# Moving one more group of channels of a depthwise convolution from VectorE to ScalarE and GpSimd, and summing its channels on VectorE, in a two-block model on one Trainium2 core

## What is computed

```python
def conformer_conv_module(h, w_in, b_in, dw, dw_b, ln_g, ln_b, w_out, b_out):
    u = h @ w_in + b_in
    u = u[..., :D_MODEL] * jax.nn.sigmoid(u[..., D_MODEL:])
    u = causal_dwconv(u, dw, dw_b)      # 31 taps, one filter per channel
    u = layer_norm(u, ln_g, ln_b)       # mean and variance over the 1024 channels
    u = jax.nn.silu(u)
    return u @ w_out + b_out
```

## Time and profile before

| | |
|---|---|
| median of 3 runs | 2315.63 us (2314.86 to 2317.98) |
| the profiled execution, its device time | 2316.43 us |
| the profiled execution, its span (first to last instruction) | 2314.6 us |
| TensorE busy | 2261.3 us, 98% |
| VectorE busy | 766.3 us, 33% |
| ScalarE busy | 430.4 us, 19% |
| GpSimd busy | 44.0 us, 2% |
| mean granted TensorE clock | 0.997 of 2.4 GHz |
| DMA | 639.71 MB, mean 276 GB/s |

### The profile page before, as it was taken

How to read it: one execution, slowest core, us unless ns; L and a number is a source line. 1 busy time by engine, 2 the same in 40 slices (tenths; PEclk the granted TensorE clock), 3 DMA queues, 4 the chain that set the end, 5 groups by cost and what they waited for, 6 DMA issues and landing times.

```text
span 2314.6 us, 31523 instructions
## 1 busy us (share of the span) xinstructions
PE 2261.3 (98%) x12908; PEld 1712.2 (74%) x12908; DVE 766.3 (33%) x1859; ACT 430.4 (19%) x1031; POOL 44.0 (2%) x66
## 2 busy tenths in 40 slices
PE   9999999999999999999999999999999999999998
PEld 8888888888888888888887885555555555555555
DVE  7944342433053441210647632222222121112212
ACT  3542210201033211110235121111111111111112
POOL 0700000000000000000000000000000000000000
PEclk9999999999999999999999999999999999999999
DMA  9644446668424444336532659999999999999996
GB/s 395 226 146 146 146 181 237 218 227 309 174 90 157 156 161 146 128 126 229 157 107 73 259 205 381 427 426 428 427 429 427 429 427 429 428 428 427 425 428 293
DMA packets 65976, 639.71 MB, mean 276 GB/s; under 512 B 7464, under 2 KB 9896, under 8 KB 12624
## 3 DMA queue, kind: packets, MB, share of 16 engines
q1 hardware_dynamic: 65872, 638.25, 69.6%
HBM read 630.86 MB, written 4.21 MB: 274 GB/s over the span
## 4 chain that ended last, share of the span: by engine, by line
PE 79%; DMA 14%; DVE 6%; issue 1%; ACT 0%; DVEq 0%; SPq 0%
PE bank L701 27%; PE bank L1283 15%; DMA arena<-in_experts 9%; PE bank L698 6%; PE bank L803 5%; PE bank L1320 5%; DMA ring<-in_experts 4%; PE bank L715 3%; PE bank L690 3%; DVE bank L2013 3%; PE bank L1274 2%; PE bank L1242 1%; PE bank L1230 1%; PE bank L814 1%; PE bank L761 1%
## 5 line engine op out<-in xcount | busy, mean ns | idle before, releaser
L701 PE MATMUL bank<-arena,ring 128*128 128x256 f32 x3136 | 680.3, 379 | 0.0
L701 PEld LDWEIGHTS bank<-arena,ring 128*128 128x128 f32 x3136 | 595.4, 190 | 80.7
L2430 DVE TENSOR_SCALAR arena<-bank 128x256 f32<-128x256 f32 x64 | 27.1, 424 | 676.2 <-PE bank L1283 676.2
L1283 PE MATMUL bank<-arena 128*64 128x256 f32 x2048 | 231.3, 380 | 12.9 <-DMA arena<-in_experts 12.8
L1283 PE MATMUL bank<-ring,arena 128*64 128x256 f32 x2048 | 234.1, 383 | 6.6 <-DMA ring<-in_experts 6.6
L1283 PEld LDWEIGHTS bank<-ring,arena 128*64 128x64 f32 x2048 | 143.3, 138 | 112.4 <-issue 30.3
L1283 PEld LDWEIGHTS bank<-arena 128*64 128x64 f32 x2048 | 144.3, 137 | 101.5 <-DMA arena<-in_experts 21.1
L698 PE MATMUL bank<-ring,arena 128*128 128x256 f32 x608 | 132.0, 379 | 0.0
L698 PEld LDWEIGHTS bank<-ring,arena 128*128 128x128 f32 x608 | 115.4, 190 | 15.6
L1732 ACT ACTIVATE arena<-arena 128x256 f32<-128x256 f32 x64 | 26.7, 416 | 532.9 <-DVE arena L2430 532.9
L803 PE MATMUL bank<-arena,ring 128*128 128x256 f32 x576 | 124.6, 379 | 0.0
(11 more groups left out here) (323 smaller groups left out, 2063.4 us busy)
## 6 DMA issues: line engine op xcount, KB each, us to landing
ring<-in_dense SPq DMA_DIRECT2D x203, 1024.0 KB, 4.9
arena<-in_experts SPq DMA_DIRECT2D x96, 2048.0 KB, 31.4
ring<-in_experts SPq DMA_DIRECT2D x87, 2048.0 KB, 30.9
ring<-in_experts SPq DMA_DIRECT2D x16, 1024.0 KB, 32.9
arena<-park SPq DMA_DIRECT2D x3, 1024.0 KB, 7.4
arena<-in_dense SPq DMA_DIRECT2D x2, 1024.0 KB, 19.1
park<-ring SPq DMA_DIRECT2D x2, 1024.0 KB, 8.2
ring<-arena SPq DMA_DIRECT2D x16, 128.0 KB, 5.6
```

The costliest lines, as they stand in the source:

```text
L701: ins = nc.tensor.matmul(o, w[:, k, j * P:(j + 1) * P], src[:, k, :], start=(k == 0), stop=(k == KT - 1))
L1283: ins = nc.tensor.matmul(o, XGT[:, k, e * CAP:(e + 1) * CAP], w[:, k, :], start=False, stop=(k == KT - 1), skip_group_check=True)
```

## The change

Chunk 5 goes from VectorE to ScalarE and GpSimd, so that VectorE has chunks 0 to 4 and the others 5 to 7. GpSimd gates the three chunks with one instruction of 768 columns and adds one tap of all three with one instruction of 768 columns, 30 in all, each by `me(...)`, waiting for itself. The ring of products stays four taps deep, now of three chunks each, in `Y` and `SQ`. ScalarE computes 93 products in place of 62, five taps behind each early unit in place of four. VectorE runs chunks 0, 1 as a pair and chunks 2, 3, 4 as a triple, with the three gatings ahead of the triple; then it adds the eight chunks into `TMP` (`channels`, seven additions, each waiting for the one before; the last three wait for GpSimd's last tap), so that TensorE needs one matmul for the mean. Of the squares of chunks 0 to 5 VectorE makes one sum (`presum`, five additions), so that TensorE needs three matmuls in place of eight. The mean's matmul stands in the middle of early unit 7, the squares' three behind the first half of unit 8.

```diff
-POOL_CHUNKS = (6, 7)
+POOL_FIRST = 5
+POOL_CHUNKS = KT - POOL_FIRST
+POOL_RING = 4
...
+        def tap_places(k):
+
+            at = (k - 1) % POOL_RING
+            return (Y, SQ)[at // 2][:, at % 2 * POOL_CHUNKS:(at % 2 + 1) * POOL_CHUNKS, :]
...
+            def channel_mean():
+
+                pe.wait_ge(sem("channels"), KT - 1)
+                nc.tensor.matmul(banks[WORK][:, 0:T], mean, TMP[:, 0:T], start=True, stop=True)\
+                    .then_inc(sem("ln_mean"), 1)
...
-            for n in range(6):
+            for n in range(EARLY - 2):
                 early(n)
-            for c in range(4):
-                channel_sum(c)
-            for n in range(6, EARLY - 1):
-                early(n)
+            early(EARLY - 2, (0,))
+            channel_mean()
+            early(EARLY - 2, (1,))
             early(EARLY - 1, (0,))
-            for c in range(4, KT):
-                ins = channel_sum(c)
-            ins.then_inc(sem("ln_mean"), 1)
-            stat("ln", 1, mean)
+            part_summed("ln", 1)
             early(EARLY - 1, (1,))
...
-            tap_products(0, 5)
-            for n in range(EARLY - 1):
+            tap_products(0, POOL_RING + 1)
+            for n in range(EARLY - 2):
                 early_out(n)
-                tap_products(5 + 4 * n, min(9 + 4 * n, TAPS))
+                tap_products(5 + 5 * n, min(10 + 5 * n, TAPS))
...
             square("ln", lambda c: U[:, c, :], "ln_centred")
+            early_out(EARLY - 2)
             root("ln", 1)
...
-            for c in POOL_CHUNKS:
+            for c in range(POOL_FIRST, KT):
                 unit_half(pool, FIRST_UNIT["cm_in"] + c, 2)
-                me.do(nc.gpsimd.tensor_tensor(G[:, c, TAPS - 1:], G[:, c, TAPS - 1:], SG[:, c, :], ALU.mult))
+            me(nc.gpsimd.tensor_tensor(G[:, own, TAPS - 1:], G[:, own, TAPS - 1:], SG[:, own, :], ALU.mult))
             for k in range(1, TAPS):
-                for i, c in enumerate(POOL_CHUNKS):
-                    pool.wait_ge(sem("tap_product"), 2 * k + i + 1)
-                    me.ended(me.n - 1)
-                    me.do(nc.gpsimd.tensor_tensor(U[:, c, :], U[:, c, :], tap_place(k, i), ALU.add))
+                pool.wait_ge(sem("tap_product"), POOL_CHUNKS * (k + 1))
+                me(nc.gpsimd.tensor_tensor(U[:, own, :], U[:, own, :], tap_places(k), ALU.add))
...
+            def channels():
+
+                me.ended()
+                for c in range(1, KT):
+                    if c == POOL_FIRST:
+                        dve.wait_ge(sem("pool_steps"), TAPS)
+                    if c > 1:
+                        dve.wait_ge(sem("channels"), c - 1)
+                    V.tensor_tensor(TMP[:, 0:T], U[:, 0, :] if c == 1 else TMP[:, 0:T], U[:, c, :], ALU.add)\
+                     .then_inc(sem("channels"), 1)
...
-            conv(0, beside)
-            glu(2)
-            glu(3)
-            conv(2, {4: [(glu, (4,)), (glu, (5,))]})
-            conv(4)
+            conv((0, 1), beside)
+            for j in range(2, POOL_FIRST):
+                glu(j)
+            conv(range(2, POOL_FIRST))
+            channels()
             dve.wait_ge(sem("ln_mean"), 1)
...
+            presum("ln", end=KT - 2, to="_part")
             r = rstd("ln", 1)
```

More of the change, by code:

```diff
@@ L779, in part_spread, with part_summed @@
                 fill(n, 4, 2 * KT)
-            def part_summed(name):
+            def part_summed(name, half=0):
                 for n, c in enumerate((0, KT - 2, KT - 1)):
@@ L787, in part_summed @@
                         pe.wait_ge(sem(name + "_part"), before(name + "_part") + KT - 3)
-                    ins = nc.tensor.matmul(banks[STAT][:, 0:T], mean, SQ[:, c, :], start=(n == 0), stop=(n == 2))
+                    ins = nc.tensor.matmul(banks[STAT][:, half * T:(half + 1) * T], mean, SQ[:, c, :],
+                                           start=(n == 0), stop=(n == 2))
                 ins.then_inc(sem(name + "_sum"), 1)
@@ L1515, in tap_products @@
                 for k in range(first, end):
[L1516 to L1524 removed]
+                    if k == 0:
+                        act.wait_ge(sem("pool_steps"), 1)
+                    elif k > POOL_RING:
+                        act.wait_ge(sem("pool_steps"), 1 + k - POOL_RING)
+                    for i in range(POOL_CHUNKS):
+                        c = POOL_FIRST + i
+                        nc.scalar.activation(tap_places(k)[:, i, :] if k else U[:, c, :], G[:, c, k:k + T], ACT.Identity,
+                                             scale=par_col("cm_dw", k * 8 + c),
                                              bias=par_col("cm_dw_b", c) if k == 0 else 0.0).then_inc(sem("tap_product"), 1)
[L1527 to L1528 removed]
+            tap_products(0, POOL_RING + 1)
+            for n in range(EARLY - 2):
                 early_out(n)
[L1530 removed]
+                tap_products(5 + 5 * n, min(10 + 5 * n, TAPS))
                 if n == 0:
@@ L1998, in glu, with conv @@
                 V.tensor_tensor(G[:, j, TAPS - 1:], G[:, j, TAPS - 1:], SG[:, j, :], ALU.mult).then_inc(sem("glu"), 1)
-            def conv(c, between={}):
-                dve.wait_ge(sem("glu"), c + 2)
+            def conv(chunks, between={}):
+                dve.wait_ge(sem("glu"), chunks[-1] + 1)
                 for k in range(TAPS):
@@ L2005, in conv @@
                         step(*arg)
-                    for i in range(2):
-                        w, src = par_col("cm_dw", k * 8 + c + i), G[:, c + i, k:k + T]
-                        kept = banks[6 + c // 2 % 2][:, i * T:(i + 1) * T]
+                    for c in chunks:
+                        w, src = par_col("cm_dw", k * 8 + c), G[:, c, k:k + T]
+                        kept = banks[6 + c // 2 % 2][:, c % 2 * T:(c % 2 + 1) * T]
                         if k == 0:
-                            me.do(V.tensor_scalar(kept, src, w, par_col("cm_dw_b", c + i), ALU.mult, ALU.add))
+                            me.do(V.tensor_scalar(kept, src, w, par_col("cm_dw_b", c), ALU.mult, ALU.add))
                             continue
-                        me.ended(me.n - 1 if k < TAPS - 1 else me.n - 1 + i)
-                        ins = V.scalar_tensor_tensor(kept if k < TAPS - 1 else U[:, c + i, :], src, w, kept, ALU.mult, ALU.add)
-                        if k < TAPS - 1:
-                            me.do(ins)
-                        else:
-                            ins.then_inc(sem("conv"), 1)
+                        me.ended(me.n - len(chunks) + 1)
+                        me.do(V.scalar_tensor_tensor(kept if k < TAPS - 1 else U[:, c, :], src, w, kept, ALU.mult, ALU.add))
+            def channels():
[7 more added lines that the diff above has]
+                     .then_inc(sem("channels"), 1)
             raw_unit(0)
```

12 lines of the change are left out of this document (2 added, 10 removed).

## The result

The changed kernel takes 2324.17 us (median of 9 runs, 2321.86 to 2324.61); the kernel before took 2316.61 beside it (9 runs, 2314.62 to 2318.68). The ratio is 1.0028, with an interval from 1.0019 to 1.0038: slower by 4.4 to 8.8 us (1.0028 is 6.5 us; the two medians themselves are 7.6 apart). The forecast was 2320.2, the range 2315 to 2326.5.

What follows compares the result with a forecast made beforehand. VectorE's convolution was taken to bound this stage before, GpSimd's additions after the change. A later mean (+1.9 us) and the clock's fall (+2.7) gave +4.6: 2320.2 us against the median 2315.63, range 2315 to 2326.5.

Steps and rivals of the forecast that it cites:

- the bounds 1.5 and 2.23: Lower and upper ends, in us, for GpSimd's addition of 768 columns; 1.83 was taken.
- rivals 1 and 2: GpSimd's 768-column addition takes 2.03: 2326 us, chance 0.16; or 1.5: 2310.6 us (2313.3 with a clock fall), chance 0.07.
- The contention term: VectorE operations with two SBUF operands delay GpSimd's additions by 0.18 us each, four channel additions counted.
- T: The time at which the mean's matmul starts on TensorE: 129.7 us, with the output product 12.2 us later.
- its 1.9: Cost of the mean's later start by itself, in us: T of 129.7 less the break-even of 127.8.
- Its two waits: TensorE's waits ahead of the second four channel sums and the sums of squares, to vanish: 2.7 us.
- the bound of 2.1: Upper end, in us, for one VectorE channel addition if it waits for GpSimd's running 768-column addition; lower end 0.51.
- The squares' chain: Centring, squares and their additions beside TensorE's two halves end at T + 6.2: no cost, 1.1 us of cover.
- The clock: TensorE's 10 us wait halves its granted clock for some five microseconds of work behind it: 2.7 us more.
- rival 3: T as forecast, but TensorE's clock stays up or returns within a microsecond or two: +1.9 to +3, 2318 us, chance 0.09.
- rival 4: The delay is swallowed before or in the phase in which weights bound: 2316 us, chance 0.06.
- of "within" and "slower": Outcomes for the whole kernel: within 0.2% of before, chance 0.46; slower by over 0.2%, chance 0.47.

Runs made afterwards that it cites:

- the version with three additions a tap: The changed kernel with GpSimd's 768-column addition split into three of 256, each waiting for the instruction before the previous one: 2328.83 us, 1.0051.
- all three profiles: The changed kernel, unaltered, profiled in three separate measurements: 2324.17, 2324.04 and 2323.11 us, ratios 1.0028, 1.0029 and 1.0027.
- wait filled: The changed kernel with twenty throwaway matmuls on TensorE in the wait ahead of the mean's matmul: 2320.73 us, 1.0014.
- The balanced version: The changed kernel with gatings early, VectorE taking chunk 5 for the last 12 taps, channel sums on TensorE in mid unit 7: 2313.31 us, 0.9983.
- the sums alone: The kernel before, chunks unmoved, with the change's channel and squares' sums on VectorE and its TensorE order: 2324.43 us, 1.0032.
- the four of higher clock above: Four of ten executions of the changed kernel with VectorE's three gatings moved into the first pair's taps: 2319.7 to 2320.3 us, mean clock 0.996 or 0.997.

## Why the prediction was right, and where it was not

Times are given from the start of the early products, 63.98 in the profile of before.

- **What bounds.** Right: GpSimd's last tap sets the mean. Its addition takes 1.82 (forecast 1.83), the reaction 0.08 (0.10). Of the bounds 1.5 and 2.23 neither was near, so rivals 1 and 2 fall by that one row. The products ahead of the first addition took 0.3 longer, and the last tap ended at 63.1 in place of 64.1: a tap was 1.906 with all that held it up, forecast 1.95. The contention term was too large for GpSimd: beside VectorE's gatings and channel additions its addition takes 1.86 to 1.88, some 0.05 more in place of 0.18. The 0.18 came from additions that overlap and holds for those: in the version with three additions a tap, three of them take 0.91 in place of 0.73 beside the gatings.
- **T.** 64.5 in all three profiles, forecast 65.7 (129.7). The wait ahead of the mean is 8.97, forecast 10.3. The way from there to the output product is 12.4 at full clock, forecast 12.2. The forecast's own balance of its 1.9 doesn't close: 10.3 less 5.2 and 2.7 is 2.4. Its two waits are 2.6 by the rows, and counted from start to start the time that TensorE lost there is 3.2, which gives the 1.9; the sum was worked out by the starts, so it isn't touched.
- **VectorE.** The three gatings took 5.78 (5.5). The fourth channel addition ended 1.69 ahead of GpSimd's last tap, where the forecast had anything from 0.3 to 6.6 ahead (and 0.5 behind by the Trainium skill's rule). The four lasted 1.77 on average, near the bound of 2.1, and each ended 0.28 behind the end of one of GpSimd's additions. So the hold-up is a wait for the running addition, as the Trainium skill has it (SBUF — State Buffer, Who interferes with whom). It was not waited for, as forecast.
- **The squares' chain** costs nothing, right: with the clock up (wait filled) VectorE ends them at 137.92 and the sums start at 139.43, 1.5 of cover where I had 1.1.
- **The clock.** Right in kind and place, full again some 4 us behind the start of the mean (forecast five). From the mean to the output product it took 14.2, 14.7 and 14.8 against 12.4 with the clock up: 1.8 to 2.4, forecast 2.7. That rules out rival 3; rival 4, a delay swallowed later, falls by the ratio. The stretch came to +2.7 to +3.3 in place of +4.6: T was 1.2 earlier and the fall 0.3 to 0.9 cheaper, less the 0.2 of the way behind T.
- **What was missed.** I took everything behind the output product as shifted but unchanged. It isn't: the clock falls behind a later wait of unchanged length, +1.7. With it the sum is +4.4 to +5.0, next to the forecast's +4.6, so that the forecast's number came near is luck: two errors cancel. The ratios say 6.2 to 6.7; 1 to 2 us of that are open, as told above. Of the 4.0 us between 2320.2 and the measured 2324.17, 1.0 is that the kernel before took 2316.61 beside the change and not 2315.63.
- The ratio, 1.0028, lies above 1.002: of "within" and "slower", which I held equally likely, it is the second, and its interval reaches just below that bound.

## What to carry to other kernels

Relieving the engine that is waited for is worth only as much as the next one in line lets through: here VectorE's taps ended 54.3 us behind the early products' start in place of 66.2, and GpSimd's self-waiting chain, with a tap of 1.9 us, took its place with an end at 63.1. Before sums are taken off a third engine and the result is thereby wanted earlier, work out when the slowest producer ends: the sums were also the cover. The balanced version, with GpSimd and VectorE ending 2 us apart and the channel sums left on TensorE, turned +0.3% into -0.2%.

A wait on TensorE has a second price, the clock behind it; throwaway matmuls in it take that price away when they end before the awaited data come, and cost their full length when they stand one place off.

## What the hardware showed that I had not expected

- **VectorE held up by a whole row of GpSimd's additions.** With GpSimd's additions 0.69 us apart and 0.73 long, each issued before the last had ended, one VectorE addition with two SBUF operands lasted 16.16 us, some 23 of GpSimd's instructions. The row of the line, with min, median and max in ns:

```profile
L2022 DVE TENSOR_TENSOR arena<-arena x7: 424/426/16157, 116.5 to 135.1; 128x256 f32<-128x256 f32 x7
```

  Where each GpSimd addition waits for the last one (the change), the longest is 1.91: VectorE gets in behind every addition.

```profile
L2020 DVE TENSOR_TENSOR arena<-arena x7: 424/1253/1911, 120.9 to 130.6; 128x256 f32<-128x256 f32 x7
```

  The Trainium skill's rule (SBUF — State Buffer, Who interferes with whom) has VectorE wait for a GpSimd instruction; this one addition waited for the whole row of them. But the unbroken row isn't enough by itself: in the same execution, beside the same row and as closely issued, the three gatings at 77.53, also with two SBUF operands, took 0.48, 0.94 and 0.95 us, and two of the kernel before 0.87 on average. What lets VectorE in at one place and not at the other, no trace here shows. VectorE's taps, with one SBUF operand, went on at full pace in both kernels.
- **A GpSimd addition by width**: 0.73 us for 256 columns, 1.275 for 512, 1.82 for 768. That is 0.545 more for every 256, which leaves 0.18 to 0.19 that doesn't grow with the width.
- **A clock that falls in one kernel and not in another**, behind the same 2.17 us wait with the same work around it: not in the two profiles of the kernel before nor with the sums alone; in the change's three and in all others but the one with the wait filled. It repeated in each profile of the kernel before and of the change, but it need not come in every execution, as the four of higher clock above suggest. With the wait filled it was gone in the one profile taken, which fits that the wait is needed for it; what else decides is open.
